# A three-layer sequence model on one core: half-width operands in the recurrent levels and in the attention values

## What is computed

```python
def step(state, inp):
    q_, k_, v_, G_, qd_, kd_, gl_ = inp
    diff = G_[..., :, None, :] - G_[..., None, :, :]
    pair_decay = jnp.exp(jnp.where(incl, diff, -jnp.inf))
    attn = jnp.einsum("bhld,bhlsd,bhsd->bhls", q_, pair_decay, k_)
    o = jnp.einsum("bhld,bhdv->bhlv", qd_, state) + jnp.einsum("bhls,bhsv->bhlv", attn, v_)
    state = gl_[..., :, None] * state + jnp.einsum("bhld,bhlv->bhdv", kd_, v_)
    return state, o
```

```python
    p = jax.nn.softmax(s, axis=-1).astype(v.dtype)
    outs.append(jnp.einsum('bhqk,bkhd->bqhd', p, v[:, :e]))
```

## Time and profile before

| | us |
|---|---|
| median of 3 runs (range) | 1730.15 (1729.68 to 1731.74) |
| the profiled execution, its own time | 1729.4 |
| its span in the profile | 1727.3 |
| of this PE busy | 1680.4 (97%) |
| HGRN2, about 754 to 1010 us | some 256 |
| attention, about 1492 to 1700 us | some 208 |

### The profile page before, as it was taken

How to read it: one execution, slowest core, us unless ns; L and a number is a source line. 1 busy time by engine, 2 the same in 40 slices (tenths; PEclk the granted TensorE clock), 3 DMA queues, 4 the chain that set the end, 5 groups by cost and what they waited for, 6 DMA issues and landing times. The chain is left out here.

```text
span 1727.3 us, 23674 instructions
## 1 busy us (share of the span) xinstructions
PE 1680.4 (97%) x8218; PEld 1368.0 (79%) x8218; DVE 1086.4 (63%) x1716; ACT 850.2 (49%) x1459; POOL 441.5 (26%) x341
## 2 busy tenths in 40 slices
PE   9998999999999999999999999999999999999997
PEld 6786787878888888778888887888888876777785
DVE  6637555477666633688788858766663367888353
ACT  6756556454333422466556545433342245455573
POOL 1444445101111200036545620111111003232231
PEclk9999999999999999999999999999999999999999
DMA  5312112322222222211121212222222221221121
GB/s 222 129 49 74 37 37 77 118 75 86 97 97 97 85 98 97 98 61 67 57 74 50 74 64 96 74 97 97 97 97 96 93 103 65 98 86 50 50 74 49
DMA packets 40372, 144.25 MB, mean 84 GB/s; under 512 B 4562, under 2 KB 4818, under 8 KB 39780
## 3 DMA queue, kind: packets, MB, share of 16 engines
q1 hardware_dynamic: 40292, 143.20, 23.4%
HBM read 141.05 MB, written 2.13 MB: 83 GB/s over the span
## 5 line engine op out<-in xcount | busy, mean ns | idle before, releaser
L190 PE MATMUL bank<-u_high,w_high 128*128 128x512 f32 x1556 | 634.2, 408 | 6.2 <-PEq L1617 1.2
L192 PE MATMUL bank<-u_high,w_low 128*128 128x512 f32 x1556 | 608.9, 391 | 0.0
L191 PE MATMUL bank<-u_low,w_high 128*128 128x512 f32 x1556 | 607.5, 390 | 0.0
L190 PEld LDWEIGHTS bank<-u_high,w_high 128*128 128x128 f32 x1556 | 293.0, 188 | 76.4 <-issue 16.0
L192 PEld LDWEIGHTS bank<-u_high,w_low 128*128 128x128 f32 x1556 | 292.2, 188 | 62.7
L191 PEld LDWEIGHTS bank<-u_low,w_high 128*128 128x128 f32 x1556 | 293.3, 188 | 56.6 <-issue 3.1
L154 ACT ACTIVATE w_high<-w_ring 128x1024 fp32r<-128x1024 f32 x228 | 239.2, 1053 | 185.6 <-PE bank L192 160.7
L163 DVE TENSOR_TENSOR w_low<-w_ring,w_high 128x1024 fp32r<-128x1024 f32 x175 | 220.2, 1263 | 159.7 <-ACT w_high L154 159.2
L163 POOL TENSOR_TENSOR w_low<-w_ring,w_high 128x1024 fp32r<-128x1024 f32 x53 | 126.8, 2402 | 343.6 <-ACT w_high L154 343.6
L928 ACT ACTIVATE conv_up<-bank,col_sb 128x512 f32<-128x512 f32 x88 | 68.6, 779 | 263.5 <-DVE bank L988 263.5
L1057 POOL TENSOR_TENSOR hidden<-conv_up 128x512 f32 x44 | 58.2, 1323 | 488.0 <-DVE conv_up L999 364.2
(11 more groups left out here) (426 smaller groups left out, 2305.0 us busy)
## 6 DMA issues: line engine op xcount, KB each, us to landing
w_ring<-ffn_up SPq DMA_DIRECT2D x88, 512.0 KB, 3.4
w_ring<-ffn_down SPq DMA_DIRECT2D x44, 512.0 KB, 3.4
w_ring<-c_in SPq DMA_DIRECT2D x32, 512.0 KB, 3.5
w_ring<-g_in SPq DMA_DIRECT2D x16, 512.0 KB, 3.8
w_ring<-m_in SPq DMA_DIRECT2D x12, 512.0 KB, 7.8
w_ring<-fox_in SPq DMA_DIRECT2D x12, 512.0 KB, 3.6
w_ring<-dsa_in SPq DMA_DIRECT2D x12, 512.0 KB, 3.4
w_ring<-ab_out SPq DMA_DIRECT2D x8, 512.0 KB, 4.0
```

The source lines that it names most:

```text
L190: nc.tensor.matmul(out, a[0], b[0], start=start, stop=False)
L191: nc.tensor.matmul(out, a[0], b[1], start=False, stop=False)
L192: return nc.tensor.matmul(out, a[1], b[0], start=False, stop=stop)
```

## The change

In `level` the stationary operand is cut to the first `keys_to` columns of the chunk: b columns fewer than 128 for b = 16 and 32 (the last block holds queries only), 66 for b = 64, all 128 for b up to 8. The moving operand is only the query blocks, 64 columns of each chunk with gaps between blocks, and the output of a chunk is 64 columns wide. `merge` reads this half-wide bank, at most 128 - b partitions for b from 16 on, and writes only the query columns of `c_attn`.

In `attention` the values lie once, not twice. `values` handles both heads of a query tile in one call: each head's 64 columns are the stationary operand, placed at column 0 or 64 of the array by `tile_position`, and each writes its own 64 rows of `b_o`. It is called at n = 2, 4, 6 and after the loop, in place of after every item. Its number of matmul instructions stays 20 for a pair. ScalarE copies the values once in full (L3161 of the new kernel); GpSimd's zeroing is gone. `high(i + 1, 2)` moves to the pair's begin, before `divide(0)`, and `high(i + 1, 3)` to n = 2.

```diff
--- before.py
+++ after.py
@@ -1113,6 +1113,12 @@
     def blocks(x, b):
         return x.rearrange("p (n e b) -> p n e b", e=2, b=b)
 
+    def late(x, b):
+        return x.rearrange("p (c n e b) -> p c n e b", c=x.shape[1] // P, e=2, b=b)[:, :, :, 1, :]
+
+    def rows(b):
+        return P - b if b >= 16 else P
+
     def x_at(h, l):
         return NL * h + l + 1
 
@@ -1176,9 +1182,13 @@
                 pe.wait_ge(x_ready, x_at(h, l))
                 if l >= 1:
                     pe.wait_ge(at_done, 8 * h + l)
+                b, half_chunk = LEVELS[l], P // 2
+                keys_to = max(rows(b), half_chunk + 2)
                 for c in range(NT):
                     xc = X[:, l % R, c * P:(c + 1) * P]
-                    ins = nc.tensor.matmul(b_x[(l + 1) % 2][:, c * P:(c + 1) * P], xc, xc, start=True, stop=True)
+                    queries = blocks(xc, b)[:, :, 1, :]
+                    out = b_x[(l + 1) % 2][0:keys_to, c * half_chunk:(c + 1) * half_chunk].rearrange("p (n b) -> p n b", b=b)
+                    ins = nc.tensor.matmul(out, xc[:, 0:keys_to], queries, start=True, stop=True)
                 ins.then_inc(lv_done, 1)
 
             def norm(h):
@@ -1471,7 +1481,10 @@
                     diff(h, l + R)
                 else:
                     nc.vector.memset(tick[:, l + R - NL:l + R + 1 - NL], 0.0)
-                nc.vector.copy_predicated(chunks(at), mask("levels", l * P).bitcast(U32), chunks(b_x[(l + 1) % 2])).then_inc(at_done, 1)
+                b = LEVELS[l]
+                new = b_x[(l + 1) % 2][0:rows(b), 0:T // 2].rearrange("p (c n b) -> p c n b", c=NT, b=b)
+                which = late(k.c("levels", l * P, l * P + P), b).to_broadcast([P, NT, P // (2 * b), b])
+                nc.vector.copy_predicated(late(at[:, :], b)[0:rows(b)], which[0:rows(b)].bitcast(U32), new).then_inc(at_done, 1)
 
             def diagonal(h):
                 take(h, 3, vraw, raw_ready)
@@ -2971,8 +2984,7 @@
     items = [(a, t) for t in reversed(range(NT)) for a in range(2)]
     qs, ks, gates = ([first, sb(f"a_{s}1", [P, T], F32)] for first, s in ((k.q0, "q"), (k.k0, "k"), (k.gate0, "gate")))
     vraw = sb("a_v_raw", [P, T], F32)
-    vp = k.sq
-    pads_zeroed = sem("a_pads_zeroed")
+    vt = k.sq[:, 0, :]
     graw = k.g_raw
     L = sb("a_logits", [P, R, T], F32)
     PT = sb("a_probsT", [P, 2, T], F32)
@@ -2990,12 +3002,6 @@
     def y_tile(i):
 
         return k.y[:, 5 + i if i < NF else 2 + i - NF, :]
-
-    def by_keys(x):
-        return x.rearrange("p (c l) -> p c l", l=P)
-
-    def padded(a):
-        return by_keys(vp[:, a, :])
 
     with nc.Block() as block:
         @block.sync
@@ -3052,18 +3058,19 @@
                 ins.then_inc(turned, 1)
 
             def values(i, n):
-                a, t = items[n]
-                pe.wait_ge(pt_ready, NI * i + n + 1)
+
+                t = items[n][1]
+                pe.wait_ge(pt_ready, NI * i + n + 2)
                 if n == 0:
                     pe.wait_ge(v_copied, i + 1)
                     if i:
                         pe.wait_ge(y_ready, i)
-                    else:
-                        pe.wait_ge(pads_zeroed, 2)
                 for j in range(t + 1):
-                    ins = nc.tensor.matmul(b_o[:, t * P:(t + 1) * P], vp[:, a, j * P:(j + 1) * P],
-                                           PT[:, n % 2, j * P:(j + 1) * P], start=a == 0 and j == 0, stop=a == 1 and j == t)
-                ins.then_inc(pv_done, 1)
+                    for a in range(2):
+                        d = slice(a * DH, a * DH + DH)
+                        ins = nc.tensor.matmul(b_o[d, t * P:(t + 1) * P], vt[:, j * P + a * DH:j * P + a * DH + DH],
+                                               PT[:, a, j * P:(j + 1) * P], start=j == 0, stop=j == t, tile_position=(0, a * DH))
+                ins.then_inc(pv_done, 2)
 
             early_products = [(j, m) for j in (0, 1) for m in (0, 1, 2)] + [(0, 3), (1, 3)] + [(j, m) for j in range(2, KD - 1) for m in range(4)]
 
@@ -3099,9 +3106,9 @@
                     if not nxt and n == NI - 1:
                         pe.wait_ge(logits_ready, NI * NP)
                         half.tile(pe, 4, (4, 5))
-                    if n:
-                        values(i, n - 1)
-                values(i, NI - 1)
+                    if n in (2, 4, 6):
+                        values(i, n - 2)
+                values(i, NI - 2)
 
             scores(0, 0)
             for i in range(NP):
@@ -3146,20 +3153,20 @@
                     nc.scalar.activation(PT[:, n % 2, 0:(t + 1) * P], b_t[:, 0:(t + 1) * P], ACT.Copy).then_inc(pt_ready, 1)
                 exp(0)
                 exp(1)
+                high(i + 1, 2)
                 divide(0)
                 act.wait_ge(v_turned, i + 1)
                 if i:
                     act.wait_ge(pv_done, NI * i)
-                nc.scalar.activation(padded(0)[:, :, 0:DH], by_keys(k.ps[3][:, :])[:, :, 0:DH], ACT.Copy)
-                nc.scalar.activation(padded(1)[:, :, DH:P], by_keys(k.ps[3][:, :])[:, :, DH:P], ACT.Copy).then_inc(v_copied, 1)
+                nc.scalar.activation(vt, k.ps[3][:, :], ACT.Copy).then_inc(v_copied, 1)
                 divide(1)
                 turn(0)
                 for n in range(2, NI):
                     exp(n)
                     if n > 2:
                         divide(n - 1)
-                    if n in (2, 3):
-                        high(i + 1, n)
+                    if n == 2:
+                        high(i + 1, 3)
                     if nxt2 and n in (4, 5):
                         high(i + 2, n - 4)
                     if i == NP - 2 and n < 7:
@@ -3189,8 +3196,6 @@
 
         @block.gpsimd
         def _(pool):
-            nc.gpsimd.memset(padded(0)[:, :, DH:P], 0.0).then_inc(pads_zeroed, 1)
-            nc.gpsimd.memset(padded(1)[:, :, 0:DH], 0.0).then_inc(pads_zeroed, 1)
             for s in (2, 3):
                 k.split_low(pool, s, 4 + s)
             with pool.Fori(2, NP + 1) as i:
```

## The result

The changed kernel takes **1719.53 us** (median of 4 runs, 1719.42 to 1720.23) against 1730.01 (4 runs, 1729.68 to 1731.74): a ratio of 0.994, 95% interval 0.9928 to 0.9951, 10.5 us less. The profiled execution took 1719.42 us, its span is 1717.6, where before they were 1729.4 and 1727.3. So the spans differ by 9.7 us. The forecast was 1716.4 us, with a range of 1710 to 1726.5.

The account below looks back on a forecast made before the run. TensorE, busy 97% of the span, was taken as the bound. Levels -6.1, values passes -13.3, entering and leaving the half mode +7.7 and early rounding -1.6 sum to -13.3 us; forecast 1716.4 us, range 1710 to 1726.5.

Parts of the forecast that it names:

- the entries: Attention values calls: entering and leaving the half-array mode costs +7.7 us, lower bound 4.3, upper 15 or 13.
- The load sets a level's pass, its moving columns don't: HGRN2 levels: only narrower weight loads at b = 16, 32, 64 shorten passes, -6.1 us; halved moving columns give 0.
- The halves run side by side, -13.3, at +7.7 for entering and leaving: Attention values: 240 passes run in 120 rounds, -13.3 us; entering and leaving the half mode adds 7.7 us.
- Early rounding, -1.6: Attention: rounding the third tile at the pair's begin removes TensorE's three waits for GpSimd's subtraction, -1.6 us.
- The two waits for ScalarE of 1.5 us in all: Forgetting attention pairs: TensorE's two waits for ScalarE, 1.5 us in all, hang on VectorE's maxima and stay.
- The new wait of ScalarE's copy at nothing: Attention: ScalarE's copy of even items now waits for earlier values calls, but fits before TensorE needs it; 0 us.
- A stall of ScalarE's copy that reaches TensorE's transposes: Sign in the attention profile that would prove the working wrong, as would a gap above 0.5 us around a values call.
- The merge at nothing: HGRN2 levels: VectorE's copies read half the columns, but VectorE isn't the bound there, so 0 us.
- halves in turns: Attention values: the array's halves take turns, -13.3 goes; 1729.4, or about 1743 with exposed loads; chance 0.12.
- a load without effect: HGRN2 levels: a narrower weight load isn't faster, so -6.1 goes; 1722.5 us, chance 0.16.
- the load not the limit: HGRN2 levels: moving columns set the pass, so all 448 passes halve, -31.8 us; 1698 us, chance 0.05.
- the change of mode at a narrow operand: HGRN2 levels: the narrower stationary operand counts as a mode change, 24 levels cost +9.6 us; 1726 us, chance 0.06.

Follow-up runs that it names:

- all 128: The changed kernel with all 128 stationary columns in every level, the moving ones staying 64: 1725.55 us.
- all 66: The changed kernel with 66 stationary columns in every level, leaving out scores of later keys, so another output: 1707.38 us.
- the third buffer: The changed kernel with three buffers for the turned probabilities in place of two, so ScalarE's copy needn't wait for the values call right ahead: 1720.03 us.
- one visit less: The changed kernel with the values of t = 1 and t = 0 in one stretch, entering the half mode three times a pair, not four: 1717.15 us.
- the last experiment: The changed kernel with ScalarE's copy ahead of the rounding, values of t = 1 and 0 together, and three first-head HGRN2 products moved earlier: 1714.33 us.
- the ninth: The changed kernel with one round of the choice of keys in place of sixteen, so another output: 1716.65 us.

## Why the prediction was right, and where it was not

The direction, the range and most of the terms held; the sum was 2.8 us too good (13.3 against 10.5 by the median; 9.7 by span). Nearly all of it is missing in the attention, 4.2 us in place of 7.2. Two slips changed nothing: 1716.1 and 0.75 are 1716.85 and not 1716.4, and the upper bound of the entries is 15 in one place and 13 in another.

1. *The load sets a level's pass, its moving columns don't*: right, shown from both sides (all 128: 0.111 us; all 66: 0.067 with the same 64 moving columns). The term was -6.1 us. The passes are 0.100, 0.089 and 0.065 us where 0.097, 0.083 and 0.057 were said, 5.2 us in all. By the Trainium skill (TensorE: Matmul & The Clock Gate, LDWEIGHTS), a load takes its columns over 1.2 GHz, an estimated 0.093, 0.080 and 0.055 us here. The passes measured are longer: their slope, (0.111 - 0.065)/62 = 0.74 ns a column, is less than the page's 0.83, and some 0.02 us of a pass doesn't go with the columns. HGRN2 is 5.95 us shorter; the 0.7 us over the passes lie in its first two heads, 0.4 and 0.3. In the first the waits changed by about as much up (GpSimd's factor) as down (a wait of 1.0 us for the state is gone), and no run tells what else did.
2. *The halves run side by side, -13.3, at +7.7 for entering and leaving*: right. A call has eight rounds for sixteen passes and 0.09 + 0.055 + 0.10 + 0.11 us around them. In the sparse pairs the two terms come to (13.3 - 7.7)/6 = 0.93 us a pair; 1.04 and 1.05 were measured, but only with the early rounding (0.83 and 0.40 without it). The values alone brought 2.2 us of the 5.6: the wait for GpSimd grew by 3.4 (1.8 to 5.2), which is the difference.
3. *Early rounding, -1.6*: too small. It is worth some 2.1 us by the stretches (2.6 by the medians), since the wait that it avoids grows as TensorE gets faster, from 1.8 to 5.2 us. It was costed as if the other edits weren't there. That it came out near 1.6 is partly luck: more than half of the 5.2 us turned up again as waits of the transposes.
4. **The step that failed** stands at the end of the same paragraph: "The two waits for ScalarE of 1.5 us in all hang on VectorE's maxima in the forgetting pairs; they stay". They didn't stay. The forgetting pairs had 0.93 us and a share of the rounding's 1.6 coming, and got 0.33, 0.56 and 0.50. In them VectorE's chain of choice steps, with ScalarE behind it, became what ends last; take the steps away and the pairs are 31.9 us like the others. The earlier trace rows had it: 29.90 of 35 us busy on VectorE in a forgetting pair, 11.81 in a sparse one. I read this 85% as room, but what counts in a chain from VectorE over ScalarE to a bank is when each link is ready, not how busy an engine is over a pair.
5. *The new wait of ScalarE's copy at nothing*: right, by the third buffer. "A stall of ScalarE's copy that reaches TensorE's transposes" was named as what would prove the working wrong, and it came (1.04 us at 1543.82), but from the other side: the copy is late behind VectorE and a rounding, not behind the values call.
6. *The merge at nothing*: nearly. VectorE's next work came to lie otherwise against GpSimd's, in part because the copies became faster, and TensorE's wait in the first head grew by 0.9 us (last section).

Of the rivals, halves in turns, a load without effect and the load not the limit are each ruled out by a run; the change of mode at a narrow operand is real at 64 columns and does not strike at 66. The Trainium skill's rule (TensorE: Matmul & The Clock Gate, Part 3, what overlaps), that a load runs beside a matmul only in other row groups, would have given an estimated 1743 us. The halves' loads, on all rows, take 0.85 us for sixteen beside eight rounds, so the trace disagrees here too:

```profile
1536.68 0.85 PEld L3071 LDWEIGHTS bank<-a_probsT,sq 128*64 128x64 f32 x16 [0.17 <-issue]
```

## What to carry to other kernels

Before halving a matmul's columns, find out from start-to-start distances which of its two sides sets the pass, load or moving columns; and if half the array is used, put the halves' passes in turns, gather them in few visits, and price each visit (0.36 us here by the rows, 0.33 and 0.42 by the run with one visit less). Price every edit against the kernel with the other edits in it: waits for a fixed supply grow as the consumer gets faster. And when the bound engine's work shrinks in a stage, follow the chain that feeds it there, even at 85% busy: half a microsecond may be all the room it has.

## What the runs showed of the hardware that was not expected

**How far halves look for each other.** Four passes apart in the list they pair as well as neighbours (4.1 rounds for 8 passes); six and eight apart they don't (8.5 rounds for 12 and 12.7 for 16, where neighbours take 6 and 8). A reach of four fits all three, but five wasn't run.

**A faster engine slowed its neighbour.** GpSimd's factor for the first head's level of b = 16, before and after, and VectorE beside it (four views, in this order):

```profile
768.29 0.91 POOL L1387 TENSOR_TENSOR c_X<-c_q,c_dif 128x256 f32<-128x256 f32 x1
```

```profile
768.87 1.71 POOL L1397 TENSOR_TENSOR c_X<-c_q,c_dif 128x256 f32<-128x256 f32 x1
```

```profile
769.18 1.21 DVE L163 TENSOR_TENSOR w_low<-w_ring,w_high 128x1024 fp32r<-128x1024 f32 x1
```

```profile
768.58 1.41 DVE L163 TENSOR_TENSOR w_low<-w_ring,w_high 128x1024 fp32r<-128x1024 f32 x1
```

VectorE's subtraction begins 0.6 us earlier, beside GpSimd's multiplication instead of behind it, and the multiplication takes 1.71 instead of 0.91 us. Half of the 0.6 us is the half-wide merge ahead of it (0.42 us, 0.73 before). The other half is an operation on c_f that the change doesn't touch, which ran at 0.48 us (0.87 before). This is not one case alone: in each of the two kernels 29 of GpSimd's 112 multiplications for the factors lie for more than half of their time beside such a subtraction, and take 1.71 us in the median (1.18 to 1.88); those with little of VectorE's work beside them take 0.72 (up to 0.92). TensorE's wait for this factor grew from 1.95 to 2.87 us. The Trainium skill (GPSIMD Engine Reference, Specifications) has GpSimd's SBUF interface shared with VectorE's instructions that read two inputs there, as this subtraction does; the trace agrees.

**The clock after that wait.** In the profile of the change TensorE stayed at its upper level behind the wait, and so it did with three buffers; in those of nine other kernels with such a wait (2.8 to 3.8 us) it did not. Behind the waits of some 1.9 us, before and with the values alone, it stayed up. Windows of 4 us of the change, then of the kernel with one visit less; the third number from the right is the granted clock:

```profile
770.00:774.00 4.00, 3.37 (x24) 3.04 (x25) 1.67 (x5) 0.90 (x2) 3.95 (x5) 1.00 0.43 131
774.00:778.00 4.00, 4.00 (x26) 3.05 (x24) 3.96 (x9) 3.94 (x6) 0.00 (x0) 1.00 0.01 2
```

```profile
770.00:774.00 4.00, 3.38 (x13) 3.00 (x14) 1.55 (x4) 0.29 (x1) 3.82 (x5) 0.54 0.40 131
774.00:778.00 4.00, 4.00 (x17) 3.33 (x16) 2.96 (x7) 3.82 (x5) 0.00 (x0) 0.61 0.01 2
```

A mean of 0.54 means that TensorE ran at the 1.2 GHz level for nearly all of the stretch; the eight microseconds hold 30 passes in place of 50. HGRN2 took 256.0 to 257.8 us in those of these profiles that have the change's levels, against 255.4 to 255.6 in the change itself and in the kernel with three buffers, where the clock stayed up too. So a wait that had cost 1.95 us became one of 2.87 with up to 2.4 us behind it, in some executions. With the wait at 0.80 us, in the last experiment, the clock stayed at 1.00 and the four runs lay within 0.3 us, where those of the ninth spread over 2.7. The runs' mean granted clocks go with it: in the ninth, 0.996 in those of 1717.53 and 1717.73 us and 0.998 in those of 1715.05 and 1715.77. That the clock is the cause of this spread wasn't tested by itself, nor what decides whether it falls behind a wait of 2.87 us.
